# Convolution's layer norm by tile, the gate's first tile in halves, the fifth embedding tile behind a gather

## What is computed

```
z = rms_norm(x) @ w_in                         # split in a_val, a_gate, b_u, b_v (512 columns each)
conv_out = depthwise_conv(a_val * sigmoid(a_gate), width 31)
ya = silu(layer_norm(conv_out))                # per token, over 512 channels
yb = gelu(b_u) * spatial_mix(layer_norm(gelu(b_v)))
h = x + concat(ya, yb) @ w_out
h = h + hierarchical_moe(rms_norm(h))          # 16 experts, 2 of them for each token
h = h + (p @ w_ple_proj) * sigmoid(rms_norm(h) @ w_ple_gate)
y = rms_norm(h)
```

## Time and profile before

| | |
|---|---|
| median of 3 runs | 689.93 us (689.25 to 692.84) |
| the profiled execution's own time | 688.93 us |
| its span, first to last instruction | 687.2 us |
| PE busy | 610.4 us (89%) |
| DVE busy | 517.2 us (75%) |
| ACT busy | 356.6 us (52%) |
| POOL busy | 193.9 us (28%) |
| mean granted TensorE clock | 0.932 of full speed |

### The profile page before, as it was taken

The page is one execution under the profiler, slowest core; times in us unless marked ns, Lnnn a source line. Parts: engine busy times, 40 slices in busy tenths (PEclk is TensorE's granted clock), DMA queues, the critical chain, the costliest instruction groups (busy, mean ns, idle before and its releaser), DMA issues.

```text
span 687.2 us, 10278 instructions
## 1 busy us (share of the span) xinstructions
PE 610.4 (89%) x3672; PEld 537.5 (78%) x3672; DVE 517.2 (75%) x568; ACT 356.6 (52%) x359; POOL 193.9 (28%) x189
## 2 busy tenths in 40 slices
PE   3899999963899999879999999999999999449994
PEld 2799999832799987668888888888888887348993
DVE  5669997998312168589999999999999999486445
ACT  6611322311613262568777777777777777424233
POOL 7144646930020000732222222222222211121004
PEclk9799999955699999999999999999999999759998
DMA  9973120235112040869999999999999999460003
GB/s 276 336 232 125 62 91 33 70 123 173 42 40 85 32 138 28 264 231 381 387 389 389 395 375 375 373 381 375 381 380 372 382 367 353 124 263 1 1 2 138
DMA packets 75659, 154.02 MB, mean 224 GB/s; under 512 B 8331, under 2 KB 25315, under 8 KB 75043
## 3 DMA queue, kind: packets, MB, share of 16 engines
q1 hardware_dynamic: 68075, 138.45, 56.8%
q0 software_dynamic: 5664, 10.08, 4.0%
q10 hardware_dynamic: 1888, 5.05, 2.2%
HBM read 147.90 MB, written 14.41 MB: 236 GB/s over the span
## 4 chain that ended last, share of the span: by engine, by line
PE 77%; DVE 10%; DMA 3%; POOL 3%; issue 3%; ACT 2%; SPq 1%; POOLq 0%; DVEq 0%; ACTq 0%
PE pair L1483 21%; PE pair L1485 21%; PE pair L1484 21%; PE pair L1535 7%; PE pair L1494 3%; DVE pair L1111 2%; DMA two<-in_state_conv 2%; POOL h L625 1%; PE pair L1751 1%; POOL h L627 1%; DVE lo L1067 1%; PE pair L1657 1%; DMA raw<-pairs 1%; ACT wide L871 1%; POOL two L609 1%
## 5 line engine op out<-in xcount | busy, mean ns | idle before, releaser
L1483 PE MATMUL pair<-hi,act_hi 128*128 128x512 f32 (+2 forms) x828 | 289.9, 350 | 14.2 <-DVE act_lo L1059 4.1
L1485 PE MATMUL pair<-hi,act_lo 128*128 128x512 f32 (+2 forms) x828 | 283.4, 342 | 0.0
L1484 PE MATMUL pair<-lo,act_hi 128*128 128x512 f32 (+2 forms) x828 | 283.3, 342 | 0.0
L1067 DVE TENSOR_TENSOR lo<-raw,hi 128x2048 fp32r<-128x2048 f32 x110 | 249.1, 2290 | 33.2 <-ACT hi L753 33.1
L753 ACT ACTIVATE hi<-raw 128x2048 fp32r<-128x2048 f32 x119 | 224.9, 1915 | 84.4 <-PE pair L1485 47.6
L1483 PEld LDWEIGHTS pair<-hi,act_hi 128*128 128x128 f32 (+1 forms) x828 | 155.5, 188 | 36.7 <-issue 11.2
L1485 PEld LDWEIGHTS pair<-hi,act_lo 128*128 128x128 f32 (+1 forms) x828 | 155.2, 187 | 18.3
L1484 PEld LDWEIGHTS pair<-lo,act_hi 128*128 128x128 f32 (+1 forms) x828 | 155.5, 188 | 16.0
L1111 DVE SCALAR_TENSOR_TENSOR pair<-conv,vecs,pair 128x512 f32<-128x512 f32 x112 | 74.8, 748 | 0.0
L676 POOL DMA_INDIRECT pairs<-two,sidx x17 | 42.9, 2525 | 111.1 <-DVE two L1350 111.1
L753 ACT ACTIVATE act_hi<-pair 128x1024 fp32r<-128x1024 f32 (+3 forms) x49 | 38.3, 792 | 53.7 <-PE pair L1494 33.7
(11 more groups left out here) (195 smaller groups left out, 519.5 us busy)
## 6 DMA issues: line engine op xcount, KB each, us to landing
raw<-in_w_exp_gate SPq DMA_DIRECT2D x34, 1024.0 KB, 7.9
raw<-in_w_exp_up SPq DMA_DIRECT2D x34, 1024.0 KB, 8.3
raw<-in_w_exp_down SPq DMA_DIRECT2D x34, 1024.0 KB, 8.7
raw<-in_w_in SPq DMA_DIRECT2D x8, 1024.0 KB, 11.9
h<-in_x_prompt SPq DMA_DIRECT2D x8, 512.0 KB, 7.0
raw<-in_w_out SPq DMA_DIRECT2D x4, 1024.0 KB, 6.0
raw<-in_w_ple_gate SPq DMA_DIRECT2D x4, 1024.0 KB, 9.5
raw<-pairs SPq DMA_DIRECT2D x4, 1024.0 KB, 8.0
```

The lines of the kernel that those rows point to most:

```text
L1067: nc.vector.tensor_tensor(lo[:, n % SPLIT, :], raw[:, n % RAW, :], hi[:, n % SPLIT, :].bitcast(F32), ALU.subtract).then_inc(lo_dve, 1)
L1483: mm(out_, x_hi, w_hi, start=start, stop=False)
L1484: mm(out_, x_hi, w_lo, start=False, stop=False)
L1485: return mm(out_, x_lo, w_hi, start=False, stop=stop)
```

## The change

**Layer norm.** DVE takes the statistics tile by tile, each with its own signal, and POOL makes each tile's inverse deviation in a pair of instructions of its own, which now also takes the maximum with 0 (`conv_deviation`). DVE's list mixes statistics, normalizing and low parts of different tiles. PE transposes tiles 0 to 2 back, then begins the output projection; tiles 3 and 4 are transposed back behind its first and second product, the state rows behind the third.

**Start of the experts.** The fifth embedding tile stands behind `transpose_gathered(0)` on PE, and its copy behind `gather_high(0)` on ACT; the embedding tiles swap the two `pair` buffers. DVE makes the low part of unit 17 (`N_STEP`) before `hidden(0)`.

**Gate.** The first tile's pair rows are loaded in two halves of 512 columns (rows of 2 KB). DVE combines and multiplies each half (`head`), PE transposes each (`head_rows`), ACT and DVE split each, and the first product waits for the second half only after its first 12 matmuls (`head_product`). For the other tiles, DVE's and ACT's lists put each tile's split ahead of the sigmoids and `gated` steps that PE's list needs later. The sigmoid table is loaded by a dummy instruction ahead.

**End.** The squares of the last tile are summed in two parts: 768 columns ahead of the last quarter's sigmoids, 256 columns at the end. POOL adds the two parts. The squares of tile 3 stand ahead of the last sigmoid instead of behind it.

The core of the diff (context and the declarations of semaphores are left out):

```diff
@@ -505,7 +513,10 @@
-            for t in range(TILES):
+            for half_of, signal in ((slice(0, C), head_in), (slice(C, D), pair_in[0])):
+                sp.dma_start(pair_rows[0].rearrange("p (k d) -> p k d", k=2)[:, :, half_of],
+                             pairs[0:2 * P, :].rearrange("(n k) d -> n k d", k=2)[:, :, half_of]).then_inc(signal, 16)
+            for t in range(1, TILES):
...
@@ -618,6 +629,16 @@
+            def conv_deviation(t):
+                r = rows(t)
+                g.wait_ge(var_done, t + 2)
+                nc.gpsimd.tensor_scalar(lr[0:r, 1, t:t + 1], mv[0:r, 1, t, 1:2], 0.0, EPS, ALU.max, ALU.add)\
+                    .then_inc(var_eps, 1)
+                g.wait_ge(var_eps, t + 2)
+                nc.gpsimd.tensor_tensor(lr[0:r, 1, t:t + 1], lr[0:r, 1, t:t + 1], half[0:r, :], ALU.pow)\
+                    .then_inc(sd_done, 1)
...
@@ -646,7 +667,8 @@
-            inverse_deviation(1)
+            for t in range(TILES):
+                conv_deviation(t)
...
@@ -736,15 +758,27 @@
+            t, r = TILES - 1, rows(TILES - 1)
+            g.wait_ge(last_sq, 1)
+            nc.gpsimd.tensor_scalar(rs[0:r, FINAL, t + 1:t + 2], sq[0:r, FINAL, t + 1:t + 2], EPS, None, ALU.add)\
+                .then_inc(eps_added, 1)
+            for t in range(TILES - 1):
...
+            t = TILES - 1
+            g.wait_ge(eps_added, 2 * TILES)
+            g.wait_ge(final_sq, t + 1)
+            nc.gpsimd.tensor_tensor(rs[0:r, FINAL, t:t + 1], rs[0:r, FINAL, t + 1:t + 2], sq[0:r, FINAL, t:t + 1],
+                                    ALU.add).then_inc(eps_added, 1)
+            g.wait_ge(eps_added, 2 * TILES + 1)
+            nc.gpsimd.tensor_tensor(rs[0:r, FINAL, t:t + 1], rs[0:r, FINAL, t:t + 1], half[0:r, :], ALU.pow)\
+                .then_inc(final_root, 1)
...
@@ -915,9 +949,13 @@
-            for t in range(TILES):
+            def embedded(t):
...
-                copy(PP[0:rows(t), t, :], pair[(0, 3)[t % 2]][0:rows(t), :]).then_inc(pp_sb, 1)
+                copy(PP[0:rows(t), t, :], pair[(3, 0)[t % 2]][0:rows(t), :]).then_inc(pp_sb, 1)
+            for t in range(TILES - 1):
+                embedded(t)
...
@@ -962,6 +1000,7 @@
+            embedded(TILES - 1)
...
@@ -1012,24 +1059,35 @@
+            nc.scalar.activation(rs[:, FINAL, TILES + 2:TILES + 3], eps[:, :], ACT.Sigmoid)
+            ps_head = pair[0][:, :].rearrange("p (c n) -> p c n", c=DC)
+            act.wait_ge(head_ps, 1)
+            copy(ahi[:, 0:CB, 0:P], ps_head[:, 0:CB, :]).then_inc(head_hi, 1)
+            act.wait_ge(xt_ps, TILES + 1)
+            copy(ahi[:, CB:, 0:P], ps_head[:, CB:, :]).then_inc(xt_hi, 1)
...
-            normed_high(0, GATE)
...
-            gate_square(2)
-            for t in range(TILES):
-                if t + 3 < TILES:
-                    gate_square(t + 3)
+            for t in range(TILES):
...
+                    if i == SPLIT - 1 and t + 2 < TILES:
+                        gate_square(t + 2)
...
-            for t in range(TILES):
+            act.wait_ge(s_add, SPLIT * TILES)
+            act.wait_ge(sq_done, 3 * TILES)
+            last_square(slice(0, SPLIT * UC), TILES, last_sq)
+            for t in range(TILES):
+                if t == TILES - 1:
+                    final_square(t - 1)
...
-                if t >= 1:
+                if 1 <= t < TILES - 1:
...
-            final_square(TILES - 1)
+            act.wait_ge(s_add, (SPLIT + 1) * TILES)
+            act.wait_ge(final_sq, TILES - 1)
+            last_square(slice(SPLIT * UC, D), TILES - 1, final_sq)
...
@@ -1193,26 +1251,51 @@
-            for t in range(TILES):
+            def conv_stats(t):
...
-                link(nc.vector.bn_aggr(mv[0:r, 1, t, :], st[0:r, 1, t, 0:6]))
-            variance(1)
-            v.wait_ge(sd_done, 2)
-            for t in range(TILES):
-                r = rows(t)
+                nc.vector.bn_aggr(mv[0:r, 1, t, :], st[0:r, 1, t, 0:6]).then_inc(var_done, 1)
+            def conv_norm(t):
+                r = rows(t)
+                v.wait_ge(sd_done, t + 2)
...
-            for t in range(TILES):
+            def conv_low(t):
...
+            def out_add(q):
+                i, t = OUT_ORDER[q]
+                at = H[0:rows(t), t, i * UC:(i + 1) * UC]
+                v.wait_ge(o_ps, q + 1)
+                nc.vector.tensor_tensor(at, bank[3 + q % 3][0:rows(t), 0:UC], at, ALU.add).then_inc(o_add, 1)
+            conv_stats(0)
+            conv_stats(1)
+            conv_stats(2)
+            conv_norm(0)
+            conv_norm(1)
+            conv_stats(3)
+            conv_norm(2)
+            conv_stats(4)
+            conv_low(0)
+            conv_norm(3)
+            conv_low(1)
+            conv_norm(4)
+            conv_low(2)
+            conv_low(3)
+            v.wait_ge(x_again, 16 * TILES)
+            out_add(0)
+            conv_low(4)
...
@@ -1353,9 +1434,9 @@
+                    split_low(N_STEP)
...
-                    split_low(N_STEP)
...
@@ -1443,24 +1524,42 @@
-            combine(0)
-            gained(0)
+            def head(half_of, arrived, one, added, made):
+                row = two[:, half_of]
+                first, second = (pair_rows[0][:, k * D + half_of.start:k * D + half_of.stop] for k in range(2))
+                v.wait_ge(arrived, 16)
+                nc.vector.scalar_tensor_tensor(out=H[:, 0, half_of], in0=first, scalar=w1[:, 0:1],
+                                               in1=H[:, 0, half_of], op0=ALU.mult, op1=ALU.add).then_inc(one, 1)
+                v.wait_ge(one, 1)
+                nc.vector.scalar_tensor_tensor(out=H[:, 0, half_of], in0=second, scalar=w2[:, 0:1],
+                                               in1=H[:, 0, half_of], op0=ALU.mult, op1=ALU.add).then_inc(added, 1)
+                v.wait_ge(added, 1)
+                nc.vector.tensor_tensor(row, H[:, 0, half_of], gain[:, half_of], ALU.mult).then_inc(made, 1)
+            v.wait_ge(gain_in, 48)
+            head(slice(0, C), head_in, head_one, head_add, head_norm)
+            head(slice(C, D), pair_in[0], pair_one, pair_add, norm_done)
+            ps_head = pair[0][:, :].rearrange("p (c n) -> p c n", c=DC)
+            v.wait_ge(head_hi, 1)
+            nc.vector.tensor_tensor(alo[:, 0:CB, 0:P], ps_head[:, 0:CB, :], ahi[:, 0:CB, 0:P].bitcast(F32),
+                                    ALU.subtract).then_inc(head_lo, 1)
+            v.wait_ge(xt_hi, TILES + 1)
+            nc.vector.tensor_tensor(alo[:, CB:, 0:P], ps_head[:, CB:, :], ahi[:, CB:, 0:P].bitcast(F32),
+                                    ALU.subtract).then_inc(xt_lo, 1)
...
-            normed_low(0, GATE)
...
-            combine(2)
-            gained(2)
-            for t in range(TILES):
-                if t + 3 < TILES:
-                    combine(t + 3)
+            for t in range(TILES):
+                if t + 2 < TILES:
+                    combine(t + 2)
+                if t + 1 < TILES:
+                    normed_low(t + 1, GATE)
+                if t + 2 < TILES:
+                    gained(t + 2)
...
-                    if i == SPLIT - 1 and t + 1 < TILES:
-                        normed_low(t + 1, GATE)
...
-                if t + 3 < TILES:
-                    gained(t + 3)
...
@@ -1633,13 +1732,20 @@
+            def state_rows():
+                pe.wait_ge(fresh_done, 1)
+                for b in range(CB):
+                    ins = tr(bank[6][0:HIST, b * P:(b + 1) * P], G[:, b, GP - HIST:GP], ident[:, :])
+                ins.then_inc(state_ps, 1)
+                for b in range(CB):
+                    ins = tr(bank[0][0:SAMPLE, b * P:(b + 1) * P], fresh[:, b, :], ident[:, :])
+                ins.then_inc(state_ps, 1)
+            pe.wait_ge(yb_mul, TILES)
+            for t in range(3):
+                conv_back(t)
...
@@ -1669,6 +1775,10 @@
+                if i == 0 and t + 3 < TILES:
+                    conv_back(t + 3)
+                if (i, t) == (0, 2):
+                    state_rows()
...
@@ -1778,8 +1887,10 @@
+            embedding(TILES - 1)
+            pe.wait_ge(pp_sb, TILES - 1)
+            step(0)
...
-            step(0)
...
@@ -1828,12 +1939,35 @@
-            gate_rows(0)
+            def head_rows(first, signal):
+                for c in range(first, first + CB):
+                    ins = tr(pair[0][:, c * P:(c + 1) * P], two[:, c * P:(c + 1) * P], ident[:, :])
+                ins.then_inc(signal, 1)
+            def head_product():
+                w_hi, w_lo = unit(N_GATE, DC)
+                for c in range(DC):
+                    if c == CB:
+                        pe.wait_ge(xt_lo, TILES + 1)
+                    ins = split_product(bank[4][:, 0:UC], ahi[:, c, 0:P], alo[:, c, 0:P], w_hi[:, c, :], w_lo[:, c, :],
+                                        c == 0, c == DC - 1)
+                ins.then_inc(s_ps, 1)
+            pe.wait_ge(head_norm, 1)
+            head_rows(0, head_ps)
+            pe.wait_ge(norm_done, 2 * TILES + 1)
```

(5 more changed lines are left out.)

36 lines of the change are left out of this document (20 added, 16 removed).

## The result

The changed kernel takes 672.02 us (median of 4 runs, 670.44 to 674.63) against 689.82 for the kernel before (4 runs, 689.25 to 692.84). The ratio is 0.9737, with a 95% interval of 0.9712 to 0.9763: 17.8 us faster. The forecast was 676.1. One execution of all those in this document, one of e7's four, ran in a slow state (716.78 us at a granted clock of 0.812), and no ratio uses it. The profiled execution took 672.32 us, with a span of 670.6 where before it was 687.2: 16.6 less.

A forecast was written before the change was run, and what follows sets the result against it. PE, with 77% of the chain, bounds the kernel; what counts is when it enters and leaves the full expert steps. Gains of 6.6 + 1.0 + 6.2 = 13.8 us off the 689.93 median give 676.1, range 670.5 to 680.5.

The forecast's parts named there:

- A: Layer norm: output projection begins 8.6 us earlier, less 2.0 for transposes between products: 6.6 us gained, bounds 5.1 and 8.4.
- The rule weighed there: Layer norm: DVE instructions with two SBUF inputs block POOL, PSUM-reading ones do not; 6.6 us if so, otherwise 5.1.
- B: First expert steps: covering the 2.45 us idle gives 0, cutting the 4.02 us gap is limited by gather 2: 1.0 us gained.
- POOL's term: First expert steps: the moved low part slows POOL's scatters, so gather 2 comes about 1 us later, out of 2.4 slack.
- C: Gate and end: earlier first product, no wait at the fourth, shorter end: 6.2 us gained, between 4.0 and 7.6.
- The head: Gate's first tile in halves: first product starts at 609.0 instead of 612.61, 3.6 us gained.
- The stall: Gate's fourth product no longer waits for the second tile's low part: 1.6 us gained, with thin cover.
- The end: Behind the last sigmoid: the last `final_norm` starts at 681.4 instead of 682.42, 1.0 us gained, between 0 and 1.5.
- Gather 2 is not late: Rival, first expert steps: full 2.3 to 3.7 us gained and clock stays up, 673.4 to 674.8 us; chance 0.12.
- The chain of tiles: Rival, layer norm: POOL pairs and splits lag, PE waits before products 1 and 2, gain falls to 3, 679.7 us; chance 0.10.
- the late first half: Rival, gate: first half comes at 605 or later, the 3.6 us gain falls to 0, 680 us; chance 0.08.
- the low clock through the products: Rival, slower than before: waits and transposes keep PE's clock low, 5.7 us per product, up to 704.6 us; chance 0.02.

The follow-up runs named there:

- e7: Changed kernel with the gate's first tile whole again (one load, undivided work), the gate's order kept as changed: 677.71 us, ratio 0.9807.
- e2: Kernel before with only the first expert steps' edits (fifth embedding tile behind the first gather's transposes, unit 17's low part moved ahead): 689.36 us, ratio 0.9973.
- e10: Changed kernel with the halves kept but DVE's and ACT's gate order behind them as before the change: 680.8 us, ratio 0.9859.
- e6: e5 with, in addition, the fifth embedding tile put back ahead of the first gather's transposes: 669.45 us, ratio 0.9682.
- e5: Changed kernel with gather 2 issued after seven of ten scatters, and the extra list's load behind step 2's weight loads: 671.8 us.
- e3: Kernel before with only the gate and end edits (halves, DVE and ACT order, last tile's squares in two parts): 683.06 us, ratio 0.9887.
- e1: Kernel before with only the layer-norm part of the change: 680.22 us, ratio 0.9825.
- e4: Changed kernel with the fifth embedding tile again ahead of the first gather's transposes; unit 17's low part stays moved: 676.16 us, ratio 0.9771.
- e8: Changed kernel with all five tiles' back-transposes and the state rows ahead of the output projection again: 676.94 us, ratio 0.9795.
- e9: Changed kernel with the first tile's pairs loaded whole by one transfer, still worked on in halves: 671.52 us, ratio 0.9741.
- e12: Changed kernel with gather 2 after seven scatters, extra list's load moved, fifth embedding tile put back, first tile's pairs loaded whole: 671.64 us, ratio 0.9747.

## Why the prediction was right, point by point

**What bounds the kernel.** Right. Stages c and e, some 363 of 687 us, did not move; all gain is in the stages of the three places named.

**A, 6.6, measured 9.1: mis-sized, and above its bound of 8.4.** The start of the projection came 9.5 us earlier (16.69 - 7.17), forecast 8.6. Normalizing began 2.54 us after the first statistics (168.41 - 165.87), forecast 3.1, because a tile's statistics take 0.85 (165.87 to 166.72) and not 1.06, which had the joint steps in it. From there to the projection it took 4.63, forecast 4.97. The roots take 0.24 + 0.58, where I took 1.21 and up to 1.31 from five columns and from a pair that DVE blocked; the forecast had them covered all the same, so this added nothing. The high clock at the first product, which I kept as the bound, came true in every kernel with the interleaved transposes. It gives 1.45, not 1.8: from the first product's start to the second's it was 4.41 us, and it is now 2.96 to the transposes behind it (the 4.7 read from the add has the way to DVE in it). The transposes between the products cost 1.5 (0.35, 0.38 and 0.79) instead of 2.0, and the three products behind them take 3.05, 2.98 and 2.95 instead of 2.88 each, 0.34 together, which the forecast lacked. The sum is 9.5 + 1.45 - 1.5 - 0.34 = 9.1.

The rule weighed there holds. POOL's power takes 0.56 to 0.58 beside statistics and normalizing, which read PSUM, and the instruction ahead of it takes 0.22 to 0.24; beside the low part L1272, which reads two SBUF tiles, that one takes 0.64. At the end of after, the powers beside `final_norm`, two SBUF inputs, take 1.91 and 1.49. The Trainium skill, GPSIMD Engine Reference, Key points, says that GpSimd contends with DVE instructions that have two SBUF inputs; the trace agrees. The scatters of the expert steps fit it too: stretched beside the weight units' low parts, not beside those that read PSUM.

**B, 1.0, measured 3.0 in after, 1.0 alone (e2) and nothing in e10.** Right are the 0 for covering 2.45 (e6 against e5; the idle time only moved ahead of the first gather's transposes), the gap of 4.02 cut to "about 1.7" (1.78, worth 2.24), and the limit by gather 2, for which PE waits 1.54 in after and 2.06 in e2. With that wait the stage ends when gather 2 lands. Before, it landed 31.8 us after the first transposes, with 2.4 of slack; in after it lands at 31.1, and 2.4 + 0.65 is the 3.0. So what was mis-sized is POOL's term: one more low part beside the scatters was to cost 1.0, and POOL issued gather 2 0.7 sooner in after (21.8 against 22.5), 0.9 later in e2 and 3.7 later in e10. That the term came out above 1.0 and not below is luck, since e10 has the same lists. The clock's part, 1.4 in step 0 and about 1.0 at the start of step 1, only makes the wait longer as long as gather 2 is late. With the early gather the term is 5.0 us (34.21 to 29.2 in e6): 2.3 from the gap, 1.6 and 1.1 from the clock in step 0 and in step 1.

**C, 6.2, measured 6.9.** The head: 3.6 forecast, 3.42 in f (3.6 in e3, 4.1 where no half is late). The stall: 1.6 forecast; e3, with the clock up as late as before, has g 1.82 less. After has 1.0 more, from the clock. In before, e1 and e2 the fourth product begins 13.25 us after the first, whether the low clock lasts 2.9 or 5.2 us, because DVE sets it; in the new order it begins after 10.5 to 12.2 without a wait, so there a sooner clock counts. The end: 1.0 forecast, 0.62; POOL's add is short (0.18) as hoped, but its power takes 1.49 beside DVE where the whole square's took 0.56. I had priced DVE's blocking for the add only.

**The halves.** The first half was forecast to be there when DVE is free. In after it was; in e4, e10, e8 and e3 it was 0.13, 0.34, 0.39 and 0.42 us late, the sign that I had called wrong. It cost little, as f shows (15.05 to 15.47 there). Where DVE waits for it, a half's rows are used 4.5 to 4.9 us after its issue (e3: 603.69 - 599.15; e4, e8, e10), a whole's after 4.7 to 5.1 (before, e1, e2, e7, e9, e12): for twice the bytes 0.3 us more in the mean. The Trainium skill, DMA: Bandwidth & Descriptors, Anatomy of one DMA — SWDGE (gpsimd) path, gives a fixed part of about 2.0 us for each transfer issued by GpSimd. These are issued by SP; the trace agrees in that a fixed part dominates, but here it is larger and the difference smaller than the 1.2 us between my two estimates from that page (3.2 and 4.4). So splitting the load buys little.

**The rivals.** "Gather 2 is not late" did not happen, and e5 and e6 show what it is worth. The chain of tiles, the late first half and the low clock through the products did not happen. The stages gained 19.0 us where 13.8 were forecast (A 2.5, B 2.0 and C 0.7 more). The profiled execution gave 2.5 of it back in stage a, and its span is 16.6 shorter; the median is 17.8 below. Without these 2.5 us it would have taken 669.9, below the range's lower end of 670.5. So the mechanisms were right, but that the time lies inside the range owes something to luck.

## What to carry to other kernels

A gap that is covered is worth only what the next waiting queue allows: ask what else must arrive at that point, and look at an engine whose list the change does not touch. Where GpSimd issues a train of transfers and the last one is waited for, look at whether each begins beside a DVE instruction with two SBUF inputs. An order that feeds the second piece in time is worth more once the first piece is early, so the two are one edit. Cut a span into stages by the starts of named instructions before a difference of a few us is explained, because three stages here moved by 1 to 3 us between kernels with the same instructions in them.

## What the runs showed of the hardware

- The granted clock that the profile prints for a window can be wrong: after's row at 28 to 30 us says 1.00 while 8 matmuls run in 2 us, as many as at 0.50 in e4. The spacing of the matmuls shows the clock.
- A wait of PE of 3.69 us ahead of eight transposes left it at the low clock (e4), one of 1.54 did not (after), nor did 2.12 in e9 (the same transposes took 1.09). Ahead of the first gather's transposes a wait of 2.66 left it there (e10, 1.66), while after one of 2.42 all stayed high (e8), and after one of 2.62 only the matmuls behind the transposes were low (e2).
- One scatter of POOL took from 0.90 to 3.09 us. Where all ten stand ahead of gather 2, its issue came from 21.8 to 26.2 us after PE's first transposes, with the same instructions on POOL in the same order. What stretches a scatter is DVE's low part of a weight unit that runs when it begins: all 51 scatters of over 1.5 us began inside one and ended 0.77 to 0.89 us after it, and none of the 89 others began over 0.03 us into one. No run moves the low parts away from the scatters, so this rests on the alignment in 14 traces.
